# A Hymba-style block on one core: the last output tile by token halves, the opening of the feed-forward in halves of three K tiles, two of its weight units converted early

## The reference

```
y   = concat(rmsnorm(y_attn, norm_attn_out), rmsnorm(y_rnn, norm_rnn_out)) @ w_out
x   = x + rmsnorm(y, norm_mix_post)
h   = rmsnorm(x, norm_ffn_pre)
y   = (gelu(causal_dwconv(h @ w_gate) + b) * (h @ w_up)) @ w_down
out = x + rmsnorm(y, norm_ffn_post)
```

## Time and profile before

| | |
|---|---|
| median of 3 runs | 2130.28 us (2129.85 to 2131.45) |
| the profiled execution | 2131.24 us |
| its span on the core | 2129.4 us |
| TensorE busy | 2116.5 us, 99% |
| VectorE busy | 1689.6 us, 79% |
| ScalarE busy | 1026.9 us, 48% |
| mean granted TensorE clock | 0.998 |

### The profile page before, as it was taken

One profiled execution on the slowest core, in us unless ns is written; L12 is line 12 of the kernel. 1 busy time (PEld: TensorE's weight loads), 2 busy tenths in 40 slices (PEclk: granted clock), 3 DMA queues, 4 the chain that ended last, 5 costly groups with the idle time before them and its releaser, 6 DMA issues.

```text
span 2129.4 us, 44272 instructions
## 1 busy us (share of the span) xinstructions
PE 2116.5 (99%) x18214; PEld 2085.7 (98%) x18214; DVE 1689.6 (79%) x2307; ACT 1026.9 (48%) x1301; POOL 353.9 (17%) x446
## 2 busy tenths in 40 slices
PE   9999999999999999999999999999999999999998
PEld 8999999999999999999999999999999999999997
DVE  7777767778855889888888888888887867767886
ACT  5565554456422555444444444444454545444543
POOL 1222323222100001111111111111211001012002
PEclk9999999999999999999999999999999999999999
DMA  5789998888643438888878888888889658679645
GB/s 178 160 191 208 201 204 199 189 198 181 166 134 93 154 119 222 223 221 212 221 215 223 224 209 220 215 223 223 228 222 281 195 154 292 178 191 277 208 139 189
DMA packets 239571, 424.90 MB, mean 200 GB/s; under 512 B 17312, under 2 KB 152352, under 8 KB 238128
## 3 DMA queue, kind: packets, MB, share of 16 engines
q0 software_dynamic: 88896, 160.49, 36.8%
q1 hardware_dynamic: 147920, 257.37, 36.8%
q10 hardware_dynamic: 2592, 4.72, 0.6%
HBM read 383.69 MB, written 89.16 MB: 222 GB/s over the span
## 4 chain that ended last, share of the span: by engine, by line
PE 98%; POOL 1%; DVE 1%; issue 0%; ACT 0%; POOLq 0%; DVEq 0%; ACTq 0%
PE bank L2115 31%; PE bank L2117 31%; PE bank L2116 30%; PE bank L2500 2%; PE bank L2207 1%; PE bank L2194 1%; PE bank L2219 0%; PE bank L2218 0%; PE bank L2234 0%; PE bank L2282 0%; PE bank L2171 0%; POOL act_lo_f L781 0%; PE bank L2300 0%; PE bank L2299 0%; POOL tsum_f L781 0%
## 5 line engine op out<-in xcount | busy, mean ns | idle before, releaser
L2115 PE MATMUL bank<-act_hi,w_all 128*128 128x256 f32 x3216 | 894.2, 278 | 0.4 <-DVE act_lo L1259 0.4
L2117 PE MATMUL bank<-act_hi,w_all 128*128 128x256 f32 x3216 | 888.4, 276 | 0.0
L2116 PE MATMUL bank<-act_lo,w_all 128*128 128x256 f32 x3216 | 888.4, 276 | 0.0
L2115 PEld LDWEIGHTS bank<-act_hi,w_all 128*128 128x128 f32 x3216 | 603.8, 188 | 7.3 <-issue 5.1
L2116 PEld LDWEIGHTS bank<-act_lo,w_all 128*128 128x128 f32 x3216 | 603.9, 188 | 0.3 <-issue 0.2
L2117 PEld LDWEIGHTS bank<-act_hi,w_all 128*128 128x128 f32 x3216 | 603.9, 188 | 0.0
L2115 PE MATMUL bank<-tsum,w_all 128*128 128x256 f32 x1312 | 362.7, 276 | 0.5 <-issue 0.5
L2117 PE MATMUL bank<-tsum,w_all 128*128 128x256 f32 x1312 | 362.1, 276 | 0.0
L2116 PE MATMUL bank<-tsum,w_all 128*128 128x256 f32 x1312 | 362.1, 276 | 0.0
L1117 ACT ACTIVATE w_all<-raw_s 128x1024 fp32r<-128x1024 f32 x176 | 186.8, 1062 | 240.0 <-PE bank L2117 229.2
L1847 DVE TENSOR_TENSOR w_all<-raw_s,w_all 128x1024 fp32r<-128x1024 f32 x176 | 215.4, 1224 | 69.8 <-ACT w_all L1117 68.6
(11 more groups left out here) (402 smaller groups left out, 3552.1 us busy)
## 6 DMA issues: line engine op xcount, KB each, us to landing
raw<-weights SPq DMA_DIRECT2D x260, 512.0 KB, 4.4
w_sums<-weights POOLq DMA_DIRECT2D x96, 512.0 KB, 7.1
raw_s<-weights SPq DMA_DIRECT2D x86, 512.0 KB, 5.3
raw_s<-weights POOLq DMA_DIRECT2D x86, 512.0 KB, 6.1
raw_a<-weights SPq DMA_DIRECT2D x67, 512.0 KB, 5.3
raw_s<-w_sums SPq DMA_DIRECT2D x48, 512.0 KB, 5.2
t_spill<-h_out POOLq DMA_DIRECT2D x48, 256.0 KB, 3.4
act_lo_f<-t_spill POOLq DMA_DIRECT2D x11, 1024.0 KB, 9.4
```

The source lines that it names most:

```text
L2115: pe.matmul(dst, ah, bh, start=start, stop=False, skip_group_check=goes_on)
L2116: pe.matmul(dst, ah, bl, start=False, stop=False, skip_group_check=goes_on)
L2117: return pe.matmul(dst, al, bh, start=False, stop=stop, skip_group_check=goes_on)
```

## The change

- Places of the weight units: opening units 0 and 1 (EARLY = 2) are transferred and converted between the units of tile 13 and those of tile 14, into a buffer of their own, `w_early`, laid over the place of `y_t`. The four units of tiles 14 and 15 come after them, each by two places later, in the same two raw slots and the same two converted slots.
- Tile 15 runs as four quarters: token half 0 over both halves of K, then token half 1 over both. All four wait at the start for the conversion of the second unit. The sums of squares of token half 0 stand inside the third quarter, its `spread` inside the fourth.
- Root, reciprocal and diagonal are made for each token half by itself (`half_root`, `invert_half`). The fillers are gone.
- The opening runs K tiles 0, 1, 2 for token half 0, then the same for half 1 (X1_STEPS), then K tiles 3 to 15 whole. The sums of squares of half 1 stand behind the first step, its spread behind the second.

The diff, cut to its core:

```diff
+EARLY = 2
+X1_STEPS = tuple((k, h) for h in range(2) for k in range(3)) + tuple((k, 2) for k in range(3, KT))
-        LAST_BANK = SB[1]
+        LAST_BANKS = ((PT[1], PT[2]), (SB[0], PT[2]))
+        ROOT_BANKS = (PJ[1], SB[2], PT[2])
+        w_early = sb_in(outp, "w_early", [EARLY, 2, UW], F32R)
```

On SyncE:

```diff
-            whole_units((N_OUT + 4) // 2, N_FF // 2)
-            for m in range(OPEN):
-                sp.wait_ge(split_done, N_FF + m - 1)
+            def opening_units(m, place):
+                sp.wait_ge(split_done, place - 1)
                 sp.dma_start(raw[:, s].rearrange("p (i n) -> p i n", i=4), four).then_inc(raw_landed[s], 16)
+            whole_units((N_OUT + 4) // 2, (N_FF - 4) // 2)
+            for m in range(EARLY):
+                opening_units(m, N_FF - 4 + m)
+            for u in range(N_FF - 4, N_FF):
+                sp.wait_ge(split_done, u + EARLY - 1)
+                sp.dma_start(raw[:, u % 2], weights[U_MIX + u]).then_inc(raw_landed[u % 2], 16)
+            for m in range(EARLY, OPEN):
+                opening_units(m, N_FF + m)
```

On ScalarE:

```diff
+            def split_early(m):
+                act.wait_ge(raw_landed[m % 2], (place - m % 2) * 8 + 16 + MORE[m % 2])
+                act.wait_ge(act_split, AFTER_Y)
+                act.activation(early(m, 0), k_tiles(raw[:, m % 2]), ACT.Copy).then_inc(hi_done, 1)
+            def split_late(u):
+                act.wait_ge(raw_landed[u % 2], (u + EARLY - u % 2) * 8 + 16 + MORE[u % 2])
+                act.wait_ge(unit_used, u - 1)
+                act.activation(w_hi[u % 2], k_tiles(raw[:, u % 2]), ACT.Copy).then_inc(hi_done, 1)
+            split(N_FF - 5, 1)
+            out_square(KT - 4)
+            split_early(0)
+            split_early(1)
+            split_late(N_FF - 4)
+            split_late(N_FF - 3)
+            out_square(KT - 3)
+            split_late(N_FF - 2)
+            split_late(N_FF - 1)
+            out_square(KT - 2)
...
+            last_square(0)
+            half_root(0, SB[2])
+            x1_hi(0)
+            x1_hi(1)
+            last_square(1)
+            x1_hi(2)
+            half_root(1, PJ[0])
+            split_opening(2)
+            for step in range(3, 6):
+                x1_hi(step)
+            for k in range(3):
+                x1_whole(k)
+            for k in range(3, KT):
+                x1_hi(k + 3)
+                x1_whole(k)
```

On VectorE:

```diff
+            split(N_FF - 5, 1)
+            out_tile(KT - 4, 0)
+            split_early(0)
+            split_early(1)
+            split_late(N_FF - 4)
+            split_late(N_FF - 3)
+            out_tile(KT - 3, 1)
+            split_late(N_FF - 2)
+            split_late(N_FF - 1)
+            out_tile(KT - 2, 2)
...
+            dve.wait_ge(last_h0_made, 1)
+            last_first(0)
+            last_second(0)
+            last_gain(0)
             dve.wait_ge(res_landed, 16 * KT)
+            invert_half(0)
+            dve.wait_ge(unit_used, N_FF - 1)
+            last_first(1)
+            dve.wait_ge(spread_done, 1)
+            for step in range(2):
+                scale_og(step)
+                add_x1(step)
+            x1_lo(0)
+            dve.wait_ge(unit_used, N_FF)
+            last_second(1)
+            x1_lo(1)
+            scale_og(2)
+            add_x1(2)
+            x1_lo(2)
+            invert_half(1)
+            dve.wait_ge(spread_done, 2)
+            scale_og(3)
+            add_x1(3)
+            scale_og(4)
+            add_x1(4)
+            x1_lo(3)
+            scale_og(5)
+            add_x1(5)
+            x1_lo(4)
+            dve.wait_ge(spread_done, 3)
+            for k in range(3, KT):
+                if k == KT - 2:
+                    last_gain(1)
+                scale_og(k + 3)
+                add_x1(k + 3)
+                x1_lo(k + 2)
                 if k >= 4 and k % 2 == 0:
                     split(N_FF + k // 2, k // 2 % 2)
```

On TensorE:

```diff
+                for half in range(2):
+                    if t == KT - 2:
+                        pe.wait_ge(split_done, N_FF - 4 + half + EARLY + 1)
+                    out_half(t, t % 4, half)
             pe.wait_ge(wo_taken, KT - 4)
-            out_half(KT - 1, 3, 0)
-            pe.wait_ge(split_done, N_FF)
+            pe.wait_ge(split_done, N_FF + EARLY)
...
+            def right_in_first(i):
+                if i == 3:
+                    pe.wait_ge(osum_ready, 1)
+                    out_sums(0, acc, True, False)
+                if i == 6:
+                    pe.wait_ge(osq_done, KT)
+                    out_sums(0, sq[:, 0], False, True).then_inc(sum_done, 1)
+            def spread_in_second(i):
+                if i == 2:
+                    spread(ROOT_BANKS[0], 1, x1_cols(0))
+            last_quarter(0, 0)
+            last_quarter(0, 1).then_inc(last_h0_made, 1)
+            pe.wait_ge(wo_taken, KT)
+            last_quarter(1, 0, right_in_first).then_inc(unit_used, 1)
+            last_quarter(1, 1, spread_in_second).then_inc(unit_used, 1)
...
-            keep_busy(3, PJ[0])
...
             pe.wait_ge(wo_taken, KT + 1)
+            x1_step(0)
+            out_sums(1, acc, True, False)
+            pe.wait_ge(osq_done, KT + 1)
+            out_sums(1, sq[:, 0], False, True).then_inc(sum_done, 1)
+            x1_step(1)
+            spread(ROOT_BANKS[1], 2, x1_cols(1))
+            pe.wait_ge(wo_taken, KT + 2)
+            spread(ROOT_BANKS[2], 2, x1_cols(2))
+            x1_step(2)
+            x1_step(3)
+            x1_step(4).then_inc(unit_used, 1)
+            x1_step(5)
+            for k in range(3, KT):
+                last = x1_step(k + 3)
```

More of the change, by code:

```diff
@@ L393, in k_tiles, with early, x1_cols @@
             return t.rearrange("p (a b n) -> p a b n", b=2, n=P)
+        def early(m, part):
+            return k_tiles(w_early[:, m, part])
+        def x1_cols(h):
+            return slice(0, S) if h == 2 else slice(HS * h, HS * h + HS)
         def w_slot(q):
@@ L1266, in invert_root, with invert_half @@
                 dve.wait_ge(rms_set, inverted)
[L1268 to L1277, removed]
+            def invert_half(h):
+                q, shape = slice(2 * h, 2 * h + 2), [P, QT // 2, P]
+                dve.wait_ge(std_done, 4 + h)
+                chain(dve.reciprocal(cols[:, 1, q], cols[:, 0, q]))
+                dve.tensor_tensor(sq[:, 0, x1_cols(h)].rearrange("p (a b) -> p a b", a=QT // 2),
+                                  ident[:].unsqueeze(1).broadcast_to(shape),
+                                  cols[:, 1, q].unsqueeze(2).broadcast_to(shape), ALU.mult).then_inc(diag_done, 1)
             def log1p_ratio(y, s, z):
@@ L1732, in _, with split_early @@
-            dve.wait_ge(spread_done, 3)
-            scale_og(1)
-            dve.wait_ge(act_hi_done, 2 * KT + 1)
-            x1_lo_half(1).then_inc(act_split, 1)
-            x1_tile(1)
-            for k in range(2, 4):
-                scale_og(k)
-                x1_lo(k - 1)
-                x1_tile(k)
-            for k in range(4, KT):
-                if k == KT - 2:
-                    dve.wait_ge(o_done, KT + 1)
-                    chain(dve.tensor_scalar(og[:, KT - 1, HS:S], o1[:, HS:S], col("g_post", KT - 1), None, ALU.mult))
-                scale_og(k)
-                x1_tile(k)
-                x1_lo(k - 1)
+            def split_early(m):
+                dve.wait_ge(hi_done, N_FF - 4 + m + 1)
+                dve.tensor_tensor(early(m, 1), k_tiles(raw[:, m % 2]), word(early(m, 0)), ALU.subtract).then_inc(split_done, 1)
@@ L2424, in _ @@
-            pe.wait_ge(wo_taken, KT - 1)
-            pe.wait_ge(osum_ready, 1)
-            for j in range(QT):
-                pe.matmul(SB[2][:, j:j + 1], acc[:, P * j:P * j + P], ones[:, 0:1], start=j == 0, stop=False,
-                          skip_group_check=True)
-            for j in range(QT):
-                if j == 0:
-                    pe.wait_ge(osq_done, KT)
-                if j == QT // 2:
-                    pe.wait_ge(osq_done, KT + 1)
-                last = pe.matmul(SB[2][:, j:j + 1], sq[:, 0, P * j:P * j + P], ones[:, 0:1], start=False, stop=j == QT - 1,
-                                 skip_group_check=True)
@@ new lines, in _, with out_sums, last_quarter @@
+            pe.wait_ge(split_done, N_FF + EARLY)
+            def out_sums(h, src, first, last):
+                bank = (SB[2], PJ[0])[h]
+                for j in range(2):
+                    ins = pe.matmul(bank[:, j:j + 1], src[:, HS * h + P * j:HS * h + P * j + P], ones[:, 0:1],
+                                    start=first and j == 0, stop=last, skip_group_check=True)
+                return ins
+            def last_quarter(h, half, within=None):
+                c, bank = x1_cols(h), LAST_BANKS[h][half]
+                for i in range(UK):
+                    if within:
+                        within(i)
+                    last = product(bank[:, c], w_tile(half, i), (act_hi[:, UK * half + i, c], act_lo[:, UK * half + i, c]),
```

(23 more changed lines are left out.)

175 lines of the change are left out of this document (68 added, 107 removed).

## The result

The changed kernel takes 2135.95 us in the median of 14 runs (2134.52 to 2138.62), the kernel before 2131.68 (2129.85 to 2133.44) in runs beside them: ratio 1.0022, 95% interval 1.0015 to 1.0030, so 4.3 us slower. It was run a second time beside later experiments: 2136.69 against 2131.17, ratio 1.0023 (1.0014 to 1.0033). The forecast was 2137.1, within 2132.5 to 2140.0. One execution in all, of 2177.79 us at a mean granted clock of 0.948 (experiment 4), belongs to a slower state and is left out wherever ratios are given.

A forecast was written before the change was run, and what follows sets the result against it. TensorE, busy 99% of the span, was taken as the bound. Waits of 2.83 and 2.58, less 1.0 gained by the order, plus 2.4 for the clock, gave +6.8 us: 2137.1 us, range 2132.5 to 2140.0.

The forecast's parts named there:

- The wait before tile 14: Early units delay the raw slot's next transfer, so TensorE waits a new 2.83 us for tile 14's first unit.
- The wait before tile 15: Tile 15 needs both units before its first product, so TensorE waits 2.58 us for the second unit's whole conversion.
- The order from tile 15 to K tile 4: From tile 15's start to K tile 4, the new order takes 28.4 us against 29.4: 1.0 us gained.
- the wait at the token halves: Between tile 15's token halves, TensorE waits 1.13 us for VectorE to take both its banks.
- The clock: Clock falls behind the waits before tiles 14 and 15: 1.2 us each on average, together 2.4, between 0 and 3.4.
- the sign named for it: Granted clock at half for some 3 us after one or both long waits, and not at the spreads.
- the clock holds: Rival: no clock fall after the waits before tiles 14 and 15; +4.4 us, 2134.7; chance 0.17.
- The forecast case, both waits with at least one fall: Waits before tiles 14 and 15 both appear and the clock falls behind at least one; chance 0.66.
- The limit on idle gaps: The skill's limit, under which both long waits stay; by it alone the clock would hold; given the smaller chance.
- the first late unit comes in time: Rival: tile 14 would not wait; +1.6 us, 2131.9, or 2133.1 with a fall at tile 15; chance 0.09.
- early conversion brings nothing: At the opening: its first unit was already converted before TensorE came to it at 710.90, so no gain.

The follow-up runs named there:

- experiment 4: Changed kernel with 11 fillers in the wait before tile 14 and 10 in that before tile 15; 2136.45 us, ratio 1.0021 to the kernel before.
- Experiment 2: Changed kernel with the first early unit ahead of tile 12's square and evacuation on ScalarE and VectorE; 2134.93 us, ratio 1.0017 to the kernel before.
- Experiment 1: Changed kernel with the last tile's wait for its second unit moved to before its second quarter; 2134.88 us, ratio 1.0014 to the kernel before.
- Experiment 3: Changed kernel with the edits of Experiment 1 and Experiment 2 together; 2131.07 us, ratio 0.9998 to the kernel before.
- experiment 6: Changed kernel with the wait for taken banks moved from before the third quarter to before the fourth; 2134.30 us in a single run.
- 7: Changed kernel with the edits of Experiment 1, Experiment 2 and experiment 6 together; 2128.65 us, ratio 0.9988 to the kernel before.
- experiment 5: The changed kernel run again without any edit; 2136.69 us, ratio 1.0023 to the kernel before.
- experiment 8: Changed kernel with Experiment 1's edit and EARLY = 0, the opening's first two units going through the usual slots; 2131.89 us, ratio 1.0005 to the kernel before.

## Why the prediction was right

- **The wait before tile 14** (2.83 forecast): 2.79 in the profile, by the chain as told, from tile 12's square through the early unit and the transfer of 3.6 us. Experiment 2 takes it away by the order of two instructions on two engines.
- **The wait before tile 15** (2.58 forecast): 2.7. The 0.1 us more is the handover from VectorE to TensorE, which the forecast left out. Experiment 1 takes it away by moving the wait behind the first quarter.
- **The order from tile 15 to K tile 4** (1.0 gained): 28.74 us from start to start against 29.42 before, 0.7 gained. With the two waits that is 4.8 of the 4.94; the other 0.1 is tile 14 itself, 10.99 us instead of 10.88. The 0.3 us short of the forecast are spread over three parts. The third quarter starts 6.76 us behind tile 15's start (6.57 forecast), the first step of the opening 7.33 behind that (7.02 forecast, with the sums and the spread inside the quarters), and K tile 4 14.65 behind the first step (14.85 forecast). So the quarters came out longer than the forecast had them, and the small waits behind them smaller: the idle marked before the first step and K tile 3 is 0.17 and 0.34, and counted as for tile 14, 0.17 more each, 0.34 and 0.51 against 0.35 and 0.65. Experiment 3 leaves 0.48 of gain, and experiments 6 and 7 show what holds it down: without the wait at the token halves it is 2.0. The forecast took that wait as given, and one moved line was enough to remove it.
- **The clock** (2.4 us forecast, 0 to 3.4): this is the term that was mis-sized. A fall costs 1.43 to 1.59 us, where the forecast gave each of two falls 1.2 on average and 1.7 at most. But in the changed kernel's first profile the sign named for it, half clock for some 3 us, did not come at all. It came in two of the four profiles that have the wait before tile 14 unfilled (experiments 1 and 5, not in that first one nor in experiment 6), and behind the wait before tile 15 in none of four (the changed kernel twice, experiments 2 and 6). By the mean clock, six of the 25 timed executions of the changed kernel look lower than the rest, and this can miss some. Six in 25 or two in four, at 1.5 us each, come to an estimate of some 0.4 to 0.8 us on average, not 2.4. The rows ahead of the prediction could not tell how often: they showed two falls and no idle time of this length without one.
- **The number itself** owes something to luck. The forecast adds 6.8 us to 2130.28, a median of three runs; the 14 runs of the kernel before beside the result have 2131.68. The change cost 4.3 us there and 5.5 in the repeat, so the sum was 2.5 and 1.3 us too high, and the low start hides 1.4 of it: 2137.1 stands 1.15 above the first median.
- The rival "the clock holds", +4.4, describes the first profiled execution and the first set of runs: stage +4.94, span +4.1, median +4.3. The forecast case, both waits with at least one fall, describes the execution profiled in the repeat, the slowest of its set: stage +6.4. The repeat's median, +5.5, lies between. The limit on idle gaps that the Trainium skill gives (TensorE: Matmul & The Clock Gate, "Why this matters for your kernels") did not hold here: the clock fell after idle 2.5 us in experiment 5 and 2.6 in experiment 1, both below it.
- The rival "the first late unit comes in time" and the forecast's remark that early conversion brings nothing fell: tile 14 waited in every profiled execution with the given order (the landing in that rival comes to 680.3 by its rows, not 680.4, which changes nothing), and experiment 8 prices the early conversion at 1.85 us. The remark looked at the order of before, where the units were ready anyway; in the new order without early units, VectorE has to convert them between the small steps that TensorE waits for.

What stays open: how often the clock falls behind waits of this length, and whether the two waits differ in that. The profiles alone would suggest it, but the mean clocks do not. Four of 11 executions lie at 0.998 in experiment 1, whose only long wait is that before tile 14, and four of 11 in experiment 2, whose only long wait is that before tile 15; none of 33 lies below 0.999 in experiments 3, 7 and 8, which have neither.

## What to carry to other kernels

Work that is put early into a chain of two slots moved every later item of that chain back here, and the price showed at the next consumer, not at the early work: follow the slot, not the engine's load. A wait belongs just ahead of the instruction that needs it; two waits moved and one pair of instructions exchanged on two engines turned this change from 5.5 us slower into 2.5 us faster, in runs side by side. When runs of a kernel spread by more than the effect, compare one stage's time between two marked instructions in the profiles.

## What the runs showed of the hardware

TensorE's granted clock fell to its lower level around idle times of 2.5 and 2.6 us in two executions (experiments 5 and 1) and held through 2.6 and 2.7 us in two others (the changed kernel and experiment 6), at the same place in the code. Once it fell about 0.3 us before the products began again, once about 0.15 us after. A fall lasted about 3.4 us (685.7 to 689.1) and cost 1.4 to 1.6 us of a full stream of matmuls, whose spacing was 0.21 us meanwhile, not 0.113.
